# Adaptive modulation in a four-layer diffusion backbone: 32 of 48 weight groups laid out by output column and summed along the row on VectorE, and some weight splits on GpSimd

## The chip, the cores and the metric

The kernel runs on one core of one Trainium2 chip. The metric is the device time of one execution in microseconds (us). The kernel before takes 3222.21 us, the median of three runs (3212.88 to 3223.43).

## What is computed

The reference is one inference step of a backbone of four layers: latent attention (layers 0 and 3), a state-space mixer (layer 1) and gated linear attention (layer 2), on 128 context tokens and 256 latent tokens of width 2048. Around each mixer stands the adaptive modulation, and that is what the change is about:

```
def ada_modulation(cond, w, b):
    m = jax.nn.silu(cond) @ w + b
    shift, scale, gate = jnp.split(m[:, None, :], 3, axis=-1)
    return shift, scale, gate
...
    for l in range(DEPTH):
        shift_p, scale_p, gate_p = ada_modulation(c_ctx[None, :], ada_w[l], ada_b[l])
        shift_s, scale_s, gate_s = ada_modulation(c, ada_w[l], ada_b[l])
        hp = rms_norm(xp, norm_pre[l]) * (1.0 + scale_p) + shift_p
        hs = rms_norm(xs, norm_pre[l]) * (1.0 + scale_s) + shift_s
        ...  (the mixer of the layer: op, os_)
        xp = xp + gate_p * rms_norm(op, norm_post[l])
        xs = xs + gate_s * rms_norm(os_, norm_post[l])
```

`ada_w` is 4 x 2048 x 6144 in float32, 201 MB. Only two condition vectors (c_ctx and c) meet it, so each of its numbers is used twice and then never again. Everything is float32.

## The kernel before, in words

**Dense weights.** Every projection is cut into chunks of four k-tiles (4 x 128 input rows) by 512 columns (384 for q). A chunk is loaded by SyncE into one of four slots of `raw`. ScalarE copies it into `w_hi` in the rounded form fp32r (`split_chunk`, L494), VectorE subtracts to get the rest, `w_lo` (L501), and TensorE runs three matmuls a tile: hi*hi, hi*lo and lo*hi (L347, or L351 for the out jobs and others whose results lie by token). `w_hi` and `w_lo` have two slots each, so ScalarE may fill the slot of chunk n once TensorE is done with chunk n-2. The semaphores are `hi_ready`, `lo_ready` and `chunk_used`. The jobs of layer 0, in order, are q0, ckv0, krope0, gate0, ukv0, out0; of layer 1 u1, gate1, glu1, out1; of layer 2 glr2, qa2, ka2, va2, r0_2, r1_2, qb2, kb2, vb2, r2_2, r3_2, out2; layer 3 repeats layer 0's. Out and gate jobs have 16 chunks.

**Modulation weights.** `ada_w` is 48 groups of 512 columns, each four slices of 1 MB. The slices pass through the same four slots of `raw` as the dense chunks, in an order fixed when the program is built (`ring_order`). SyncE's queue loads strictly in that order, and each load waits until the slot's last user is done (`load_chunk`, L302). There are two ways through:

- Multiplied: 27 groups. TensorE multiplies a slice by the padded conditions (L386, four matmuls of 32 output rows side by side, `pe_ada_part`), ScalarE copies the sums out of bank 4 (`act_ada`), and TensorE turns them so that columns lie on partitions (L401, `pe_ada_turn`). Groups 0 to 15 go at the start and beside q0, the other 11 beside gate1, qa2, ka2, va2, r0_2, vb2 and r2_2 (`ada_after`).
- Summed apart: 21 groups. VectorE multiplies each k-tile by one number per partition and adds to a running sum, once for each condition (L432, `dve_ada_step`: 32 instructions a group), spread over the dense chunks by `summed_apart`. At the end TensorE sums over the partitions and turns, with eight matmuls by a column of ones (L412, `pe_ada_take`). The slot of the last slice is held until then.

VectorE then adds the bias into `mod` (`dve_ada`, L465).

`stream` (L510) gives the order within VectorE and ScalarE for one dense job: for each chunk first the split of the next chunk, then the modulation steps, then what else the stage has (`between`). VectorE and every other engine run strictly in their written order. GpSimd issues DMAs only, and a few memsets.

## Time and profile before

| | |
|---|---|
| median of three runs | 3222.21 us |
| the profiled execution, its own time | 3231.19 us |
| its span (first to last instruction) | 3229.1 us |
| TensorE busy | 3059.2 us, 95% |
| VectorE busy | 1908.1 us, 59% |
| ScalarE busy | 1050.1 us, 33% |
| GpSimd busy | 203.9 us, 6% |
| DMA | 636 MB, mean 197 GB/s |
| TensorE's granted clock, mean | 0.975 of 2.4 GHz |

The span is one execution seen by the hardware profiler, and lies 2.1 us inside that execution's own time. "Busy" for TensorE is a union of overlapping matmuls, and says that work stood there, not that it ran at its peak. VectorE's and ScalarE's instructions hardly overlap, so that their busy time is close to their load; back-to-back instructions start a little earlier than the one before ends. An engine's share is a mean over stages, and the stages differ.

### The profile page before, as it was taken

Reading aid. Unit: us, or ns where it says so; the run is one execution under the profiler, and the core shown is the slowest. Engines: PE = TensorE matmul, PEld = TensorE weight load, DVE = VectorE, ACT = ScalarE, POOL = GpSimd, SP = SyncE. Lnnn points to the kernel's source line nnn. Section 1 sums busy time; section 2 is a strip of 40 time slices with the busy share of each in tenths; the row PEclk is TensorE's granted clock in tenths of the full one; section 3 lists DMA queues with packets and bytes.
Section 4 is the critical chain, followed back from the end, with each engine's and each line's share of the span. In section 5 each row is a group of like instructions: output and inputs, shape, how many; then the busy total and the mean of one; then the engine's idle time right before and its main releaser. Section 6 shows DMA issues by size and latency. Waiting matters only on the chain.

```text
span 3229.1 us, 46744 instructions
## 1 busy us (share of the span) xinstructions
PE 3059.2 (95%) x19631; PEld 2651.0 (82%) x19631; DVE 1908.1 (59%) x2811; ACT 1050.1 (33%) x1409; POOL 203.9 (6%) x321
## 2 busy tenths in 40 slices
PE   5799999999999999889998999999999999999998
PEld 2588889977788989779987877987787999987777
DVE  3499985545767734638775363764475775235443
ACT  1333333233324222232324243324324222323332
POOL 1034340000000210000000000000000000000000
PEclk7899999999999999989999999999999999999999
DMA  9889995411455897866654564555363655431132
GB/s 354 323 309 352 344 334 182 164 49 53 156 183 179 246 257 270 334 244 219 226 183 142 178 220 164 200 205 191 129 226 126 212 196 176 131 95 53 53 131 91
DMA packets 290498, 636.01 MB, mean 197 GB/s; under 512 B 22000, under 2 KB 55424, under 8 KB 281584
## 3 DMA queue, kind: packets, MB, share of 16 engines
q1 hardware_dynamic: 264384, 524.58, 47.4%
q0 software_dynamic: 25904, 108.44, 9.7%
q8 instruction: 154, 2.52, 0.3%
q14 instruction: 56, 0.46, 0.0%
HBM read 561.01 MB, written 71.89 MB: 196 GB/s over the span
## 4 chain that ended last, share of the span: by engine, by line
PE 80%; DMA 7%; DVE 7%; ACT 3%; DVEq 2%; issue 1%; ACTq 1%; POOL 0%; SPq 0%; POOLq 0%
PE bank L347 36%; PE bank L351 21%; DMA raw<-in_ada_w 3%; PE bank L881 3%; PE bank L875 3%; PE bank L386 2%; PE bank L896 2%; DVE w_lo L501 2%; DVE arena L2147 1%; PE bank L922 1%; PE bank L2518 1%; DMA raw<-in_mla_w_in 1%; PE bank L412 1%; DMA raw<-in_s_w_in 1%; PE bank L900 1%
## 5 line engine op out<-in xcount | busy, mean ns | idle before, releaser
L501 DVE TENSOR_TENSOR w_lo<-raw,w_hi 128x2048 fp32r<-128x2048 f32 (+2 forms) x352 | 617.7, 1771 | 697.7 <-ACTq L495 694.2
L494 ACT ACTIVATE w_hi<-raw 128x2048 fp32r<-128x2048 f32 (+2 forms) x352 | 520.4, 1496 | 1246.8 <-PE bank L347 612.7
L347 PE MATMUL bank<-hT_hi,w_hi 128*128 128x384 f32 (+1 forms) x2608 | 898.4, 344 | 22.3 <-ACT scratch L981 7.7
L347 PE MATMUL bank<-hT_lo,w_hi 128*128 128x384 f32 (+1 forms) x2608 | 885.9, 340 | 0.0
L347 PE MATMUL bank<-hT_hi,w_lo 128*128 128x384 f32 (+1 forms) x2608 | 885.8, 340 | 0.0
L347 PEld LDWEIGHTS bank<-hT_hi,w_hi 128*128 128x128 f32 (+1 forms) x2608 | 492.5, 189 | 49.9 <-issue 34.3
L347 PEld LDWEIGHTS bank<-hT_lo,w_hi 128*128 128x128 f32 (+1 forms) x2608 | 492.5, 189 | 1.5 <-issue 0.5
L347 PEld LDWEIGHTS bank<-hT_hi,w_lo 128*128 128x128 f32 (+1 forms) x2608 | 492.2, 189 | 1.4 <-issue 0.6
L351 PE MATMUL bank<-w_hi,hT_hi 128*128 128x512 f32 x1056 | 421.9, 399 | 3.1 <-issue 2.9
L351 PE MATMUL bank<-w_hi,hT_lo 128*128 128x512 f32 x1056 | 418.1, 396 | 0.0
L351 PE MATMUL bank<-w_lo,hT_hi 128*128 128x512 f32 x1056 | 417.9, 396 | 0.0
L566 ACT ACTIVATE arena<-bank 128x512 f32<-128x512 f32 (+6 forms) x285 | 145.4, 530 | 349.6 <-PE bank L386 80.9
L351 PEld LDWEIGHTS bank<-w_hi,hT_hi 128*128 128x128 f32 x1056 | 199.9, 189 | 58.2 <-issue 13.4
L351 PEld LDWEIGHTS bank<-w_hi,hT_lo 128*128 128x128 f32 x1056 | 199.7, 189 | 46.8
L351 PEld LDWEIGHTS bank<-w_lo,hT_hi 128*128 128x128 f32 x1056 | 200.0, 189 | 44.9
L432 DVE SCALAR_TENSOR_TENSOR bank<-raw,silu_pad,bank 128x512 f32<-128x512 f32 x294 | 221.1, 752 | 21.5 <-issue 8.8
L432 DVE SCALAR_TENSOR_TENSOR arena<-raw,silu_pad,arena 128x512 f32<-128x512 f32 x294 | 219.6, 747 | 0.0
L386 PE MATMUL bank<-raw,silu_pad 128*32 128x512 f32 x864 | 122.7, 647 | 34.9 <-DMA raw<-in_ada_w 34.5
L2147 DVE TENSOR_TENSOR arena<-arena 128x896 f32<-128x896 f32 (+1 forms) x128 | 142.4, 1154 | 5.9 <-issue 4.4
L881 PE MATMUL bank<-w_hi,hT_hi 128*128 128x256 f32 x512 | 99.4, 288 | 3.2 <-DVEq L857 1.6
L875 PE MATMUL bank<-hT_hi,w_hi 128*128 128x512 f32 x256 | 86.5, 419 | 8.1 <-DVE hT_hi L1231 4.3
L1241 DVE TENSOR_REDUCE small<-bank 128x1 f32<-128x384 f32 (+1 forms) x96 | 39.1, 463 | 89.2 <-PE bank L900 87.3
(338 smaller groups left out, 2922.1 us busy)
## 6 DMA issues: line engine op xcount, KB each, us to landing
raw<-in_ada_w SPq DMA_DIRECT2D x192, 1024.0 KB, 7.3
raw<-in_mla_w_in SPq DMA_DIRECT2D x64, 768.0 KB, 7.5
raw<-in_gla_w_in SPq DMA_DIRECT2D x48, 1024.0 KB, 7.4
raw<-in_mla_w_in SPq DMA_DIRECT2D x40, 1024.0 KB, 5.3
raw<-in_mla_w_out SPq DMA_DIRECT2D x32, 1024.0 KB, 5.2
raw<-in_s_w_in SPq DMA_DIRECT2D x32, 1024.0 KB, 8.6
s_out_dram<-arena POOLq DMA_DIRECT2D x32, 512.0 KB, 5.8
s_in_dram<-arena POOLq DMA_DIRECT2D x16, 1024.0 KB, 9.6
```

Of the source, the lines that this page charges most:

```text
L347: mm = nc.tensor.matmul(banks[m][0:width, 0:TOK], wp[:, k, at:at + width], hp[:, kt, :], start=(first and n == 0), stop=(last and n == 2))
L351: mm = nc.tensor.matmul(banks[m][:, 0:cols], hp[:, kt, m * P:(m + 1) * P], wp[:, k, 0:cols], start=(first and n == 0), stop=(last and n == 2))
L386: mm = nc.tensor.matmul(banks[4][32 * k:32 * k + 32, :], silu_pad[:, at:at + 32], raw_of("ada", a, s)[:, k, :], start=(s == 0), stop=(s == ...
L432: op = nc.vector.scalar_tensor_tensor(out=raw_of("ada", a, s)[:, c, :] if k == 15 else sums, in0=got, scalar=by, in1=sums, op0=ALU.mult, o ...
L494: nc.scalar.activation(dst, src_, ACT.Copy)
L501: nc.vector.tensor_tensor(dst, src_, pick(w_hi, *part)[0], ALU.subtract)
L566: return nc.scalar.activation(out, in_, ACT.Copy)
L875: mm = nc.tensor.matmul(banks[7][:, 0:KEYS], wp[:, slot, kt, j * 256:j * 256 + P], cp[:, kt, :], start=(kt == 0 and m == 0), stop=(kt == 3 ...
L881: mm = nc.tensor.matmul(banks[7][:, (t % 2) * 256:(t % 2 + 1) * 256], cp[:, kt, t * P:(t + 1) * P], wp[:, slot, kt, :].rearrange("p (h x) ...
L896: nc.tensor.matmul(score_bank(hh, t), qn[:, 2 * pair + hh, at], kT[:, pair % 2, hh, a:b], start=True, stop=False, skip_group_check=True)
L1241: nc.vector.reduce_max(mx[h % 2][:, t:t + 1], score_bank(h, t), AX.X)
L2147: nc.vector.tensor_tensor(to, powers, f, ALU.mult)
```

## The change

Groups 0 to 15 stay as they were, multiplied by TensorE. The other 32, in nine sets of three or four (`summed_sets`), are all treated on VectorE, and in another way:

- The host lays their weights out by output column (`ada_rows`): a partition holds 4 pieces of 512 input rows for one output column and a quarter of the inputs, 8 KB in one stretch. Loading is a plain copy of 1 MB a slice.
- SiLU of the two conditions is written once to DRAM and read back, broadcast over partitions (`pool_silu`), into a place in the arena for each set, or for sets 5 to 7 for one condition into PSUM bank 4.
- VectorE multiplies a piece of 512 by the conditions element by element and sums along the row in the same instruction (`accum_out`), one number per partition: again 32 instructions a group (1024 in all, against 672 L430 and L432 before).
- At the end of a set TensorE adds the four quarters of the inputs, with four matmuls of 32 output rows (`spread`), nine times.
- Five stages (gate0, out0, glu1, out1, out2) have their `w_lo` subtraction on GpSimd for all but the first chunk or two: 15, 15, 14, 15 and 15 chunks, 74 in all (`by_pool`, `pool_splits`).
- ScalarE's last gate copies in layer 0 wait for set 0 to be summed, because the conditions' place lies in the gate's area; GpSimd's `fetch_x` in layer 1 waits for set 3.

```diff
--- before.py
+++ after.py
-ADA_READ = (7, 11, 17, 19, 26, 31, 41, 43, 47)
-ADA_TURNED_APART = (7, 11, 15, 26, 36, 41)
+ADA_TENSOR = 16
+ADA_READ = (7, 11, 15)
...
+    return {("q0", g): ADA_START + g for g in range(ADA_TENSOR - ADA_START)}
+def summed_sets(layers):
+    def chunks(name, first, end):
+        per = chunks_of(name)
+        return [(name, n // per, n % per) for n in range(first, end)]
+    gla = [(f"{name}2", n, s) for name, groups in GLA_ORDER for n in range(groups) for s in range(4)]
+    return [(range(16, 20), chunks("gate0", 0, 16), (13824, 14336, 22144)),
+            (range(20, 23), chunks("out0", 1, 13), (12928, 13632, 13448)),
+            (range(23, 27), chunks("u1", 1, 16) + chunks("gate1", 0, 11), (4608, 5120, 5632)),
+            (range(27, 31), chunks("glu1", 1, 16), (19200, 19712, 20224)),
+            (range(31, 34), chunks("out1", 1, 13), (12928, 13632, 13448)),
+            (range(34, 38), gla[:24], (12928, None, 13448)),
+            (range(38, 41), gla[28:47], (12928, None, 13448)),
+            (range(41, 44), chunks("out2", 1, 13), (12928, None, 13448)),
+            (range(44, 48), chunks("q3", 1, 31), (9216, 9728, 10240))]
...
+    steps, loads, dense = {}, {}, dense_order(layers)
+    for groups, keys, _ in summed_sets(layers):
         for n, a in enumerate(groups):
             for k in range(16):
-                key = keys[(16 * n + k) // pace]
+                key = keys[(16 * n + k) * len(keys) // (16 * len(groups))]
                 steps.setdefault(key, []).append((a, k))
                 if k % 4 == 0:
                     loads.setdefault(dense[dense.index(key) + 1], []).append((a, k // 4))
-            takes[key] = a
...
+            if a >= ADA_TENSOR:
+                load_chunk(sp, "ada", a, s, w["ada_rows"][a // ADA_LAYER, 4 * (a % ADA_LAYER) + s], GC)
+                return
...
-        def pe_ada_take(pe, a):
-            pe.wait_ge(ada_summed, 32 * (SUMMED.index(a) + 1))
-            if a - 1 in ADA_READ:
-                pe.wait_ge(ada_turned, a + ada_reads(a))
-            for c in range(2):
-                for j in range(4):
-                    at = 8 * (a % ADA_LAYER) + 2 * j + c
-                    mm = nc.tensor.matmul(banks[5][:, at:at + 1], raw_of("ada", a, 3)[:, c, j * P:(j + 1) * P], one_col,
-                                          start=True, stop=True)
+        def pe_ada_take(pe, f):
+            groups, _, places = SETS[f]
+            pe.wait_ge(ada_summed, sums_before(groups[-1]) + 33)
+            pe.wait_ge(ada_turned, set_taken(f) - 1)
+            n = 8 * len(groups)
+            for k in range(4):
+                mm = nc.tensor.matmul(banks[5][32 * k:32 * k + 32, 0:n], spread[:, :], sums_of(f)[:, k, 0:n],
+                                      start=True, stop=True, skip_group_check=True)
             mm.then_inc(ada_turned, 1)
+        def sums_of(f):
+            return view(SETS[f][2][2], 4, 32)
+        def silu_of(f, c):
+            at = SETS[f][2][c]
+            return banks[4][:, :] if at is None else view(at, GC)
...
-            n, s, kk = SUMMED.index(a), k // 4, k % 4
-            if kk == 0:
+            s, f = k // 4, SET_OF[a]
+            first = a == SETS[f][0][0]
+            if k % 4 == 0:
                 chunk_landed(nc.vector, "ada", a, s)
-            if k == 0 and a in (16, 44):
-                x_free(nc.vector, a // ADA_LAYER - (a == 16))
-            if k == 0 and a - 1 not in SUMMED:
-                nc.vector.wait_ge(ada_turned, a + ada_reads(a))
-            for c, sums in enumerate((banks[4][:, :], ada_rows(a))):
-                got, by = raw_of("ada", a, s)[:, kk, :], silu_c[:, k, c:c + 1]
-                if n or k:
-                    nc.vector.wait_ge(ada_summed, 32 * n + 2 * k + c - 1)
-                if k == 0:
-                    op = nc.vector.tensor_scalar(sums, got, by, None, ALU.mult)
-                else:
-                    op = nc.vector.scalar_tensor_tensor(out=raw_of("ada", a, s)[:, c, :] if k == 15 else sums, in0=got, scalar=by,
-                                                        in1=sums, op0=ALU.mult, op1=ALU.add)
-                op.then_inc(ada_summed, 1)
+            if k == 0 and first:
+                nc.vector.wait_ge(ada_turned, set_taken(f) - 1)
+                if f in SILU_PLACED:
+                    nc.vector.wait_ge(silu_in, 16 + 64 * (SILU_PLACED[f] + 1))
+            for o in (2 * (k % 4), 2 * (k % 4) + 1):
+                kk, c = ((0, 0), (1, 0), (0, 1), (2, 0), (1, 1), (3, 0), (2, 1), (3, 1))[o]
+                done = sums_before(a) + 8 * s + o
+                if done > (o != 1):
+                    nc.vector.wait_ge(ada_summed, done - (o != 1))
+                got = raw_of("ada", a, s)[:, kk, :]
+                at = 8 * (a - SETS[f][0][0]) + 2 * s + c
+                nc.vector.scalar_tensor_tensor(out=got if c else banks[5][:, :], in0=got, scalar=1.0, in1=silu_of(f, c), op0=ALU.mult,
+                                               op1=ALU.mult, accum_out=sums_of(f)[:, kk, at:at + 1]).then_inc(ada_summed, 1)
+            if k == 15 and a == SETS[f][0][-1]:
+                nc.vector.drain().then_inc(ada_summed, 1)
...
+        def pool_silu(pool, r):
+            c0, c1, _ = SETS[[f for f in SILU_PLACED if SILU_PLACED[f] == r][0]][2]
+            to = view(c0, 2, c1 - c0)[:, :, 0:GC]
+            for q in range(4):
+                nc.gpsimd.dma_start(to[32 * q:32 * q + 32, :, :],
+                                    silu_dram[:, q * GC:(q + 1) * GC].unsqueeze(0).broadcast_to([32, 2, GC])).then_inc(silu_in, 16)
...
+            elif eng == "pool":
+                nc.gpsimd.wait_ge(hi_ready, n + 1)
+                nc.gpsimd.wait_ge(lo_ready, n)
+                for part in parts:
+                    dst, src_ = pick(w_lo, *part)
+                    nc.gpsimd.tensor_tensor(dst, src_, pick(w_hi, *part)[0], ALU.subtract).then_inc(lo_ready, 1)
             else:
                 nc.vector.wait_ge(hi_ready, n + 1)
+                if by_pool(n - 1):
+                    nc.vector.wait_ge(lo_ready, n)
...
+        def by_pool(n):
+            name, g, s = dense[n] if n >= 0 else ("", 0, 0)
+            return 4 * g + s >= {"gate0": 1, "out0": 1, "glu1": 2, "out1": 1, "out2": 1}.get(name, 99)
+        def pool_splits(name, first, end):
+            for n in range(first, end):
+                split_chunk("pool", name, n // 4, n % 4)
...
                     if g == 0:
                         pe_spread_gate(pe, l, s)
+                    if (g, s) == (3, 1) and l != layers[-1]:
+                        pe_ada_take(pe, (1, 4, 7)[l])
...
+                if (l, g) == (0, 3):
+                    act.wait_ge(ada_summed, sums_before(19) + 33)
+                if (l, g) == (3, 0):
+                    act.wait_ge(ada_turned, set_taken(8))
...
+            if l == 2:
+                dve.wait_ge(norm_taken[0], 8 * n + 7)
+                nc.vector.tensor_copy(banks[4][:, :], silu_of(4, 1))
...
             if l != layers[0]:
                 pool.wait_ge(x_added, NT * (parked(l) - 1))
+                if l != 2:
+                    pool_silu(pool, {1: 2, 3: 5}[l])
                 nc.gpsimd.dma_start(x_dram.rearrange("t p d -> p t d"), x).then_inc(x_saved, 16)
                 pool.wait_ge(x_saved, 16 * (parked(l) - 1))
         def fetch_x(pool, l):
             pool.wait_ge(h_lo_ready, h_quarter(f"mix{l}", 3))
+            if l < 2:
+                pool_silu(pool, (1, 4)[l])
+            if l == 1:
+                pool.wait_ge(ada_turned, set_taken(3))
...
+            pool.wait_ge(scanned, 2)
+            pool_silu(pool, 3)
             nc.gpsimd.dma_start(outs[4].rearrange("a b d (g h) n r -> (a b d g) (h n r)", h=2), st_rows)\
                 .then_inc(state_stored, 16)
+            pool_splits(f"glu{l}", 2, 16)
...
+                if l != layers[-1]:
+                    pool_splits(f"out{l}", 1, 2)
                 fetch_x(pool, l)
+                if l != layers[-1]:
+                    pool_splits(f"out{l}", 2, 16)
...
+            if l == 0:
+                x_free(pool, l)
+                pool_silu(pool, 0)
+                pool_splits("gate0", 1, 5)
             pool.wait_ge(kv_normed, nth(l) + 1)
             nc.gpsimd.dma_start(outs[2][0, j], ckv_sb[:, 0, :]).then_inc(stored, 16)
+            if l == 0:
+                pool_splits("gate0", 5, 13)
             pool.wait_ge(kr_taken, nth(l) + 1)
             nc.gpsimd.dma_start(outs[3][0, j], kr_sb[:, 0, 0:ROPE]).then_inc(stored, 16)
+            if l == 0:
+                pool_splits("gate0", 13, 16)
...
+    by_column = arrays["ada_w"].reshape(DEPTH, 4, GC, 48, 4, 32).transpose(0, 3, 1, 5, 4, 2)
+    arrays["ada_rows"] = np.ascontiguousarray(by_column).reshape(DEPTH, 48, P, 4, GC)
```

On TensorE, in gate1 (layer 1), between two dense chunks. L401 and L386 are the turn and the multiplication of a modulation group, L2480 is the state-space mixer's own work, L347 the dense matmuls. Before:

```order
L401 MATMUL bank<-small,arena 128x2 x4
L386 MATMUL bank<-raw,silu_pad 32x512 x4
L2480 MATMUL bank<-arena 64x50 x32
L347 MATMUL bank<-hT_hi,w_hi 128x384
L347 MATMUL bank<-hT_lo,w_hi 128x384
```

And now (L2568 and L357 are the same two lines of code in the changed file):

```order
L2568 MATMUL bank<-arena 64x50 x32
L357 MATMUL bank<-hT_hi,w_hi 128x384
L357 MATMUL bank<-hT_lo,w_hi 128x384
L357 MATMUL bank<-hT_hi,w_lo 128x384
```

The modulation has left the place between the chunks.

On VectorE, in gate0 (layer 0), around one dense chunk late in the stage. L501 is the `w_lo` split, L432 the modulation, L813 to L819 the attention's keys. Before:

```order
L501 TENSOR_TENSOR w_lo<-raw,w_hi 128x2048
L432 SCALAR_TENSOR_TENSOR bank<-raw,silu_pad,bank 128x512
L432 SCALAR_TENSOR_TENSOR arena<-raw,silu_pad,arena 128x512
L432 SCALAR_TENSOR_TENSOR bank<-raw,silu_pad,bank 128x512
L432 SCALAR_TENSOR_TENSOR arena<-raw,silu_pad,arena 128x512
L813 TENSOR_TENSOR arena<-bank,arena 128x256 x2
L816 TENSOR_TENSOR arena<-arena 128x256 x2
L819 TENSOR_TENSOR arena<-arena 128x256 x2
```

And now (L449 is the modulation, L878 to L884 the keys):

```order
L449 SCALAR_TENSOR_TENSOR bank,arena<-raw,arena 128x512 x2
L449 SCALAR_TENSOR_TENSOR raw,arena<-raw,arena 128x512
L449 SCALAR_TENSOR_TENSOR bank,arena<-raw,arena 128x512
L449 SCALAR_TENSOR_TENSOR raw,arena<-raw,arena 128x512
L449 SCALAR_TENSOR_TENSOR bank,arena<-raw,arena 128x512
L449 SCALAR_TENSOR_TENSOR raw,arena<-raw,arena 128x512 x2
L878 TENSOR_TENSOR arena<-bank,arena 128x256 x2
L881 TENSOR_TENSOR arena<-arena 128x256 x2
L884 TENSOR_TENSOR arena<-arena 128x256 x2
```

Eight modulation instructions stand between one chunk's keys and the next, and the split is gone from this engine.

On GpSimd, in layer 0 from the rotary tables on. Before:

```order
L2757 DMA arena<-const_rope_swap 128x128
L2759 DMA out<-arena 128x512
L2761 DMA out<-arena 128x64
L1807 DMA arena<-in_x_prompt 128x2048
L1808 DMA arena<-in_x_sample 128x2x2048
L1800 DMA x_saved_dram<-arena 128x3x2048
```

And now:

```order
L2855 DMA arena<-const_rope_swap 128x128
L470 DMA arena<-silu_dram 32x2x512 x4
L541 ISA
L541 TENSOR_TENSOR w_lo<-raw,w_hi 128x2048 x4
L2861 DMA out<-arena 128x512
L541 TENSOR_TENSOR w_lo<-raw,w_hi 128x2048 x8
L2865 DMA out<-arena 128x64
L541 TENSOR_TENSOR w_lo<-raw,w_hi 128x2048 x4
L470 DMA arena<-silu_dram 32x2x512 x4
L1890 DMA arena<-in_x_prompt 128x2048
L1891 DMA arena<-in_x_sample 128x2x2048
L541 TENSOR_TENSOR w_lo<-raw,w_hi 128x2048 x14
```

The splits of gate0 and out0 stand among the DMA issues, and one of out0's stands ahead of the second group of condition loads.

## Rows read from the trace of the kernel before

**Rows 1.** The page, part 1: busy us, share of the span, instructions.

```profile
PE 3059.2 (95%) x19631; PEld 2651.0 (82%) x19631; DVE 1908.1 (59%) x2811; ACT 1050.1 (33%) x1409; POOL 203.9 (6%) x321
```

**Rows 2.** The page, part 4: the chain of waits, shares by engine.

```profile
PE 80%; DMA 7%; DVE 7%; ACT 3%; DVEq 2%; issue 1%; ACTq 1%; POOL 0%; SPq 0%; POOLq 0%
```

**Rows 3.** Windows (gate0, out0, glu1's stream, out2): length, busy PE, PEld, DVE, ACT, POOL.

```profile
498.10:643.10 145.00, 144.23 (x833) 143.03 (x833) 87.41 (x107) 43.21 (x42) 1.09 (x2) 1.00 0.50 169
815.90:980.40 164.50, 158.09 (x735) 127.98 (x734) 106.64 (x132) 50.14 (x58) 1.27 (x2) 0.98 0.49 173
1446.70:1586.10 139.40, 138.91 (x802) 138.58 (x800) 111.30 (x122) 44.25 (x35) 0.55 (x1) 1.00 0.57 198
2316.00:2467.80 151.80, 147.59 (x689) 121.69 (x688) 99.28 (x114) 45.95 (x46) 0.77 (x1) 0.99 0.51 182
```

**Rows 4.** Timeline of TensorE in gate1: start, length, line, what, count.

```profile
1205.99 0.95 PE L401 MATMUL bank<-small,arena 128*128 128x2 f32 x8
1206.88 1.07 PE L386 MATMUL bank<-raw,silu_pad 128*32 128x512 f32 x8
1207.87 2.07 PE L2480 MATMUL bank<-arena 128*64 128x50 f32 x64
```

**Rows 5.** Timeline of TensorE in out0, between two dense chunks.

```profile
940.61 1.84 PE L412 MATMUL bank<-small,raw 128*128 128x1 f32 x16
942.31 0.48 PE L351 MATMUL bank<-w_hi,hT_hi 128*128 128x512 f32 x1
```

**Rows 6.** Groups by line, VectorE and TensorE: count | busy us, mean ns | idle before.

```profile
L412 PE MATMUL bank<-small,raw 128*128 128x1 f32 x336 | 40.0, 249 | 4.1 <-DVE raw L432 4.1
L501 DVE TENSOR_TENSOR w_lo<-raw,w_hi 128x2048 fp32r<-128x2048 f32 x216 | 495.0, 2292 | 630.0 <-ACTq L495 627.1 <-issue 0.9
L432 DVE SCALAR_TENSOR_TENSOR bank<-raw,silu_pad,bank 128x512 f32<-128x512 f32 x294 | 221.1, 752 | 21.5 <-issue 8.8 <-DMA raw<-in_ada_w 6.4
L432 DVE SCALAR_TENSOR_TENSOR arena<-raw,silu_pad,arena 128x512 f32<-128x512 f32 x294 | 219.6, 747 | 0.0
L2194 DVE SCALAR_TENSOR_TENSOR arena<-arena 128x512 f32<-128x512 f32 x32 | 21.9, 686 | 0.0
```

**Rows 7.** Timeline of VectorE in out0, around one dense chunk.

```profile
918.54 2.29 DVE L501 TENSOR_TENSOR w_lo<-raw,w_hi 128x2048 fp32r<-128x2048 f32 x1 [1.38 <-ACTq L495]
921.02 0.76 DVE L432 SCALAR_TENSOR_TENSOR bank<-raw,silu_pad,bank 128x512 f32<-128x512 f32 x1 [0.19 <-issue]
921.68 0.75 DVE L432 SCALAR_TENSOR_TENSOR arena<-raw,silu_pad,arena 128x512 f32<-128x512 f32 x1
922.35 0.75 DVE L432 SCALAR_TENSOR_TENSOR bank<-raw,silu_pad,bank 128x512 f32<-128x512 f32 x1
```

**Rows 8.** Timelines in out0: two hi splits, and TensorE's first matmul of each chunk.

```profile
916.57 1.92 ACT L494 ACTIVATE w_hi<-raw 128x2048 fp32r<-128x2048 f32 x1 [0.16 <-issue]
924.15 1.92 ACT L494 ACTIVATE w_hi<-raw 128x2048 fp32r<-128x2048 f32 x1 [5.66 <-PE bank L351]
...
923.89 0.39 PE L351 MATMUL bank<-w_hi,hT_hi 128*128 128x512 f32 x1
932.25 0.40 PE L351 MATMUL bank<-w_hi,hT_hi 128*128 128x512 f32 x1
```

**Rows 9.** The lines L1006 and L1814: duration min/median/max ns, first and last start.

```profile
L1006 ACT ACTIVATION_READ_ACCUMULATOR arena<-bank x48: 191/194/195, 873.6 to 3221.5; 128x1 f32 x48
L1814 POOL MEMSET arena<- x1: 1802/1802/1802, 1762.4 to 1762.4; 32x2048 f32 x1
```

**Rows 10.** Timeline of ScalarE at the end of gate0.

```profile
638.87 1.92 ACT L494 ACTIVATE w_hi<-raw 128x2048 fp32r<-128x2048 f32 x1 [6.96 <-PE bank L347]
647.26 0.49 ACT L1056 ACTIVATE arena<-bank 128x384 f32<-128x384 f32 x1 [1.61 <-PE bank L347]
```

**Rows 11.** Timeline of TensorE at the end of glu1.

```profile
1586.28 1.84 PE L412 MATMUL bank<-small,raw 128*128 128x1 f32 x16
1591.03 0.76 PE L351 MATMUL bank<-w_hi,hT_hi 128*128 128x512 f32 x1 [2.91 <-issue]
```

138 lines of the change are left out of this document (76 added, 62 removed).

## The prediction, as it stood before the result

> **What bounds the kernel now.** I read the page's busy shares first: TensorE is busy 95% of the span, VectorE 59%, GpSimd 6% and almost only with DMA issues [rows 1]. Then the chain of waits: 80% of the path that sets the end is TensorE's [rows 2]. Then windows by stage: in gate0, out0, the dense stream of glu1, and out2 TensorE idles 0.8, 6.4, 0.5 and 4.2 us [rows 3]. So every microsecond taken from TensorE in a dense stage counts, as long as nothing else becomes the pacemaker. Who is next can be read from the same windows: VectorE, with 87 of 145, 107 of 165, 111 of 139 and 99 of 152 us [rows 3].
>
> **What leaves TensorE.** Eleven groups are no longer multiplied there. In gate1 the multiplication of one slice holds TensorE from 1206.88 to 1207.87, 1.0 us, and the turn of a group from 1205.99 to 1206.88, 0.9 us [rows 4]: 11 x (4 x 1.0 + 0.9) = 54 us. The 21 takes (336 records, 16 each [rows 6]) go too: the dense matmul behind one starts 1.70 us after it [rows 5], and two of them also waited for VectorE, 4.1 us in all: 21 x 1.7 + 4 = 40 us. Nine new takes of four matmuls come in, nearest to the turn: 9 x 0.9 = 8 us. Net 54 + 40 - 8 = 86 us, all on the path. ScalarE's eleven copies go as well, off the path.
>
> **What the new VectorE instruction costs.** Before, the instructions of L432 start 0.66 us apart (921.02, 921.68, 922.35 [rows 7]) and last 752 ns, pointer scalar included; one without such a scalar lasts 686 ns [rows 6], which makes 0.60 apart. The sum has to be read out in addition, and no row of VectorE shows that. From below it costs nothing; from above I take ScalarE's readout, 194 ns [rows 9], on top of the slower form: 0.60 to 0.86 us. I take 0.75. The new chain also waits once in eight for the instruction just ahead, 0.2 us as behind a split [rows 7]. A slice is thus 8 x 0.75 + 0.2 = 6.2 us, and gate0, out0, out1 and out2 have one a chunk, glu1 slightly more.
>
> **What the split costs on GpSimd.** It is 2292 ns on VectorE [rows 6]; there are 74 that move. GpSimd has no such instruction in the trace. Its memset of 2048 numbers takes 1802 ns [rows 9], so one stream of that length costs it 1.8 us; a subtraction has two coming in and one going out. Ends: 1.8 us (all three side by side) and 5.4 us (one after another). I take 4.5, nearer the upper end, as two inputs surely share something. The time there is for it: in out0 the hi split that starts at 916.57 ends at 918.49 and TensorE takes up that chunk at 923.89, 5.4 us later, and the next has 926.07 to 932.25, 6.2 us [rows 8]. The first is the case in which ScalarE was held by its squares. So 4.5 us fits beside TensorE with 0.8 us over, and the upper end just fits too. Without this cover every microsecond over some 5.5 to 6.2 would cost one for each of the 74 chunks.
>
> The Trainium skill (GPSIMD Engine Reference, 3.1 Elementwise) has this subtraction's like, two inputs of 2048 float32, at 4497 ns. No row here shows it. By that page the sum would be what it is.
>
> **VectorE's pace where it is tightest.** In out0 a chunk takes TensorE 8.36 us (923.89 to 932.25 [rows 8]). VectorE's own work there is 106.6 - 16 x 2.29 - 64 x 0.66 = 28 us, 1.7 a chunk [rows 3]; 6.2 + 1.7 = 7.9 us, just under. In gate0: 87.4 - 16 x 2.29 - 52 x 0.66 = 16 us, 1.0 a chunk; 7.2 us under 8.9 (145 us less two takes, by 16). In the other sets a chunk has 4.3 to 5.3 modulation instructions and keeps its split, about what it had. Unevenness within the out stages should still cost something: 0.86 us apart instead of 0.75 is 0.9 us a chunk, 0.4 over. I charge 5 us.
>
> **New waits.** (a) End of gate0: the hi split of the next job ends at 640.79 [rows 10], VectorE's split of it then ends near 643.1 and the last slice near 649.4; only then may ScalarE make its four last gate copies (2 us, so 651.4, against 647.75 before [rows 10]). Behind them in ScalarE's queue is the split of the latents that TensorE waits for: 3.7 us. (b) End of glu1: VectorE has eight or nine instructions of 0.75 behind its last split where it had six of 0.66, 2.3 us more, and behind them stands the gating that out1's first chunk needs; TensorE already waited there until 1591.03 [rows 11]: 2 us. (c) At the start of the out jobs GpSimd splits a chunk, then issues up to six DMAs at 0.6 us, then splits the next: 2 us in out0, less elsewhere. (d) The loads of SiLU lie ahead of x's in GpSimd's queue, and VectorE waits for them before its first step of a set; a slice waits in its slot, so I allow 2 us. SyncE gains a little: the slot of a group's last slice comes free with VectorE and no longer with TensorE. Sum of costs: 5 + 4 + 2 + 2 + 2 = 15 us.
>
> **The sum.** 3231.2 (the profiled execution's own time; its span is 2.1 less) - 86 + 15 = 3160 us. That execution stood 9 us above the median of 3222.2, so in the median's terms 3151.
>
> **The rivals.**
>
> 1. *VectorE and GpSimd get in each other's way; slower than before.* Each new modulation instruction reads two inputs from SBUF, and so does each split that moves. If the two engines reach SBUF through something they share, and an instruction holds it from start to end, the times add. Then a chunk costs VectorE 6.2 + 4.5 = 10.7 us. Out0 and out1: eight chunks at 8.36 and four at about 10.2, 2.3 x 8 + 0.5 x 4 = 20 each. Gate0: 10.7 + 1.0 - 8.9 = 2.8, by 15: 42. Glu1: 11.1 - 8.4 = 2.7 by 14, and the gating (three of 1.75): 42. Out2, with one condition's numbers in PSUM, may hide one instruction a chunk: 13. Together 137 us: 3151 + 137 = 3288. It decides from the point where 6.2 plus what is taken away exceeds a chunk, 2.2 us of the 4.5. For it: a two-input instruction needs twice the reading, and VectorE is loaded in just these five stages. Against: nothing in the trace; GpSimd's DMA issues show no stretch, but they do not read tiles. This is the largest risk.
>
> The Trainium skill (SBUF — State Buffer, "SBUF: two separate sides") states just this: whichever of a VectorE instruction with two SBUF inputs and a GpSimd instruction that reads SBUF starts first has the pair of ports to itself until it ends. By that rule the case above holds in full. No run here has yet shown it.
>
> 2. *The readout makes the new instruction much dearer*, about 1.2 us: twice 512 elements' time, (0.60 + 0.53). Then 9.8 us a slice; by the same chunks, out0, out1 and out2 some 20 each, gate0 31, glu1 31, and q3, where 128 such instructions stand beside 32 splits in 233 us, 19: 141 us and 3292. For it: there is no row. Against: two SBUF inputs alone do not do it (L432 takes 747 ns with both in SBUF, 752 with one in PSUM [rows 6]).
>
> The Trainium skill (Vector Engine (DVE) Microarchitecture Reference, 7. Points that are easy to get wrong) says that this form with two sources that are not bf16 in SBUF halves the throughput, since nothing is left to read the accumulator back. No row here has an accumulating instruction on VectorE, so this rival rests on it.
>
> 3. *GpSimd is slower than I take*, 6.5 to 7 us a split: 74 x 0.5 to 1.2 = 37 to 90 us given back, 3190 to 3240, around no change. For it: the interleaving with six DMA issues and fp32r output. Against: one stream costs 1.8 us.
>
> **How the numbers follow.** Forecast 0.48; rival 1 0.34; rival 2 0.05; rival 3 0.09; some other small net effect 0.04. The range of the forecast alone is 3135 to 3185, from 0.60 and 0.86 us for the instruction and none or twice the waits. For 8 in 10 the range has to reach rivals 1 and 3: 3138 to 3305; rival 1's own width (0.60 to 0.86 us, 3.6 to 5.4 us) is 3240 to 3350, so that its upper part is left out. A measurement of this kernel tells 0.3%, 10 us, from no change. Faster by more: 0.48 + 0.02 + 0.02 = 0.52. Slower by more: 0.34 + 0.05 + 0.03 = 0.42. The same: 0.06. I set the time at 3155, 4 us above the sum, for waits I have not found.
>
> **What the profile after would show.** TensorE: no L386 behind q0, nine takes of about 0.9 us, chunks of out0 8.36 us apart where no take stands. VectorE: the new instruction with its readout, 0.75 us from pair to pair. GpSimd: splits of 4.5 us that do not change when VectorE is busy, and VectorE's instructions the same in gate1 (no split on GpSimd) as in gate0. If instead the modulation instructions in the five stages show single ones of several microseconds, or GpSimd's splits stretch when VectorE runs, rival 1 holds; if all of them last 1.2 us, in q3 too, rival 2. If SyncE's loads in out0 wait for VectorE and ScalarE's hi splits wait for a DMA, VectorE has become the pacemaker there, and the forecast is wrong.

## The result, and the profile after

The changed kernel takes 3259.83 us (median of four runs, 3255.62 to 3261.70) against 3217.55 us for the kernel before beside it: ratio 1.0133, 95% interval 1.0107 to 1.0159. The forecast was 3155 us: 2% faster was foretold, and the kernel is 1.3% slower. The time lies inside the range (3138 to 3305), on the side of rival 1.

The page after, part 1 (answers to [rows 1]):

```profile
PE 2958.5 (91%) x18927; PEld 2594.9 (80%) x18927; DVE 2190.0 (67%) x4117; ACT 1043.5 (32%) x1399; POOL 570.3 (18%) x420
```

TensorE is busy for 101 us less. The span grew by 29 us all the same (3258.5 against 3229.1; by the medians it is 42, the profiled execution of the kernel before being 14 us above its median), so TensorE's idle time grew by 130. The chain of waits, which was 80% TensorE's [rows 2], shows who took over:

```profile
PE 58%; DVE 24%; DMA 8%; ACT 4%; issue 2%; DVEq 2%; ACTq 1%; POOL 1%; SPq 0%; POOLq 0%
```

Windows after of gate0, out0, glu1 (whole) and out2, columns as in [rows 3]:

```profile
488.20:648.70 160.50, 147.42 (x821) 144.24 (x820) 155.62 (x276) 42.65 (x40) 71.69 (x17) 0.97 0.57 203
824.90:1010.60 185.70, 155.75 (x711) 126.71 (x711) 129.37 (x246) 50.14 (x58) 75.61 (x21) 0.93 0.50 178
1320.60:1594.80 274.20, 234.99 (x3111) 218.48 (x3109) 206.69 (x510) 85.65 (x108) 72.19 (x21) 0.95 0.68 256
2361.60:2513.70 152.10, 143.83 (x673) 119.80 (x672) 116.69 (x226) 45.92 (x47) 70.77 (x16) 0.97 0.58 209
```

The columns are: the window and its length, busy time of PE, PEld, DVE, ACT and POOL, the granted clock, the DMA share and GB/s. Length minus TensorE's busy time is its idle time: 13 us in gate0 (0.8 before), 30 in out0 (6.4), 39 in glu1 (22.7, also for the whole stage), 8 in out2 (4.2). VectorE is busy 97% of gate0. Now one chunk of out0: VectorE, then GpSimd in the same microseconds (answers to [rows 7]).

```profile
900.77 0.70 DVE L449 SCALAR_TENSOR_TENSOR bank<-raw,arena 128x512 f32<-128x512 f32 x1
901.39 0.14 DVE L449 DVE_READ_ACCUMULATOR bank<-raw,arena 128x1 f32 x1
901.39 0.69 DVE L449 SCALAR_TENSOR_TENSOR raw<-raw,arena 128x512 f32<-128x512 f32 x1
902.00 5.10 DVE L449 SCALAR_TENSOR_TENSOR bank<-raw,arena 128x512 f32<-128x512 f32 x1
907.02 0.13 DVE L449 DVE_READ_ACCUMULATOR bank<-raw,arena 128x1 f32 x1
907.02 0.68 DVE L449 SCALAR_TENSOR_TENSOR raw<-raw,arena 128x512 f32<-128x512 f32 x1
...
911.45 4.92 DVE L449 SCALAR_TENSOR_TENSOR bank<-raw,arena 128x512 f32<-128x512 f32 x1
```

```profile
901.50 5.04 POOL L541 TENSOR_TENSOR w_lo<-raw,w_hi 128x2048 fp32r<-128x2048 f32 x1 [6.15 <-ACTq L534]
910.70 5.11 POOL L541 TENSOR_TENSOR w_lo<-raw,w_hi 128x2048 fp32r<-128x2048 f32 x1 [4.16 <-ACTq L534]
```

The same instruction takes 0.69 us alone and 5.10 us when it starts while a split runs: it ends about 0.6 us after the split does, its own time. It goes the other way too. The split at 901.50 started while VectorE's instruction of 901.39 was still running (to 902.08), and ended 4.46 us after it. Of the 74 splits 54 started during a modulation instruction with both inputs in SBUF, and from the end of that one to the end of the split it is 4.46 us in the median. So whichever starts second waits for the first. But such an instruction lasts 0.7 us and a split 4.6, so VectorE pays nearly all of it. That is rival 1 in one picture. By groups (count | busy us, mean ns):

```profile
L449 DVE SCALAR_TENSOR_TENSOR bank<-raw,arena 128x512 f32<-128x512 f32 x512 | 505.3, 987 | 59.3 <-DMA arena<-silu_dram 23.0 <-DMA raw<-in_ada_rows 19.9 <-issue 11.4
L449 DVE SCALAR_TENSOR_TENSOR raw<-raw,arena 128x512 f32<-128x512 f32 x352 | 305.0, 884 | 4.1 <-issue 0.4
L449 DVE SCALAR_TENSOR_TENSOR raw<-raw,bank 128x512 f32<-128x512 f32 x160 | 106.2, 682 | 3.6 <-issue 0.5
L541 POOL TENSOR_TENSOR w_lo<-raw,w_hi 128x2048 fp32r<-128x2048 f32 x74 | 354.0, 4784 | 649.9 <-ACTq L534 649.9
```

The two forms with both inputs in SBUF have means of 987 and 884 ns; the one whose second input is in PSUM stays at 682. Of the 864 of the two forms 53 last over 2 us, at most one for each of the 74 splits: 12 in gate0, 8 in out0, 13 in glu1, 11 in out1 and 9 in out2. Against the medians VectorE spends 219 us more on them. The split costs 4.78 us on the average, its waits included; 4.5 was assumed.

There is a second loss, which no rival named. TensorE's waits in layer 2, 1879 to 2092 and 2233 to 2362 us (us, times, longest), where the kernel before had none and GpSimd splits nothing:

```profile
PE bank L1514 <- DVEq L1766: 18.1, 2, 9.2
PE bank L361 <- DVEq L550: 11.7, 6, 3.6
...
PE bank L1514 <- DVEq L1766: 19.2, 2, 9.7
```

L1766 is the linear attention's decayed keys. They stand behind a chunk's modulation steps on VectorE. L550 is the end of a `w_lo` split on VectorE, in va2.

### The profile page after: what moved, and what is told of

Same layout as the page of the kernel before. It is cut to its first block, busy times and chain, and to the rows that moved or that the text cites. A ratio compares the mean times of both kernels' runs of the same rounds, so it can differ in the third digit from the quotient of the medians.

```text
span 3258.5 us, 46791 instructions
## 1 busy us (share of the span) xinstructions
PE 2958.5 (91%) x18927; PEld 2594.9 (80%) x18927; DVE 2190.0 (67%) x4117; ACT 1043.5 (32%) x1399; POOL 570.3 (18%) x420
## 4 chain that ended last, share of the span: by engine, by line
PE 58%; DVE 24%; DMA 8%; ACT 4%; issue 2%; DVEq 2%; ACTq 1%; POOL 1%; SPq 0%; POOLq 0%
PE bank L357 28%; PE bank L361 12%; DVE bank L449 10%; DVE raw L449 5%; DMA raw<-in_ada_w 3%; PE bank L946 3%; PE bank L940 3%; DVE w_lo L549 2%; PE bank L961 2%; PE bank L987 1%; DMA raw<-in_ada_rows 1%; PE bank L2606 1%; ACT w_hi L533 1%; PE bank L965 1%; DVE arena L2230 1%
## 5 line engine op out<-in xcount | busy, mean ns | idle before, releaser
L357 PE MATMUL bank<-hT_hi,w_hi 128*128 128x384 f32 (+1 forms) x2608 | 889.2, 341 | 33.8 <-POOL w_lo L541 11.2
L357 PE MATMUL bank<-hT_hi,w_lo 128*128 128x384 f32 (+1 forms) x2608 | 878.4, 337 | 0.0
L357 PE MATMUL bank<-hT_lo,w_hi 128*128 128x384 f32 (+1 forms) x2608 | 878.1, 337 | 0.0
L549 DVE TENSOR_TENSOR w_lo<-raw,w_hi 128x2048 fp32r<-128x2048 f32 (+3 forms) x278 | 448.1, 1632 | 444.7 <-ACTq L534 441.0
L449 DVE SCALAR_TENSOR_TENSOR bank<-raw,arena 128x512 f32<-128x512 f32 x512 | 505.3, 987 | 59.3 <-DMA arena<-silu_dram 23.0
L357 PEld LDWEIGHTS bank<-hT_hi,w_hi 128*128 128x128 f32 (+1 forms) x2608 | 493.7, 189 | 53.9 <-issue 23.3
L357 PEld LDWEIGHTS bank<-hT_lo,w_hi 128*128 128x128 f32 (+1 forms) x2608 | 493.5, 189 | 1.2
L357 PEld LDWEIGHTS bank<-hT_hi,w_lo 128*128 128x128 f32 (+1 forms) x2608 | 493.0, 189 | 1.1
L541 POOL TENSOR_TENSOR w_lo<-raw,w_hi 128x2048 fp32r<-128x2048 f32 x74 | 354.0, 4784 | 649.9 <-ACTq L534 649.9
L449 DVE SCALAR_TENSOR_TENSOR raw<-raw,arena 128x512 f32<-128x512 f32 x352 | 305.0, 884 | 4.1 <-issue 0.4
L624 ACT ACTIVATE arena<-bank 128x512 f32<-128x512 f32 (+5 forms) x274 | 138.9, 527 | 363.8 <-PE bank L394 63.4
L449 DVE SCALAR_TENSOR_TENSOR raw<-raw,bank 128x512 f32<-128x512 f32 x160 | 106.2, 682 | 3.6 <-issue 0.5
L394 PE MATMUL bank<-raw,silu_pad 128*32 128x512 f32 x512 | 75.0, 670 | 33.3 <-DMA raw<-in_ada_w 32.6
```

The costliest lines, as they stand in the source:

```text
L357: mm = nc.tensor.matmul(banks[m][0:width, 0:TOK], wp[:, k, at:at + width], hp[:, kt, :], start=(first and n == 0), stop=(last and n == 2))
L394: mm = nc.tensor.matmul(banks[4][32 * k:32 * k + 32, :], silu_pad[:, at:at + 32], raw_of("ada", a, s)[:, k, :], start=(s == 0), stop=(s == ...
L449: nc.vector.scalar_tensor_tensor(out=got if c else banks[5][:, :], in0=got, scalar=1.0, in1=silu_of(f, c), op0=ALU.mult, op1=ALU.mult, acc ...
L541: nc.gpsimd.tensor_tensor(dst, src_, pick(w_hi, *part)[0], ALU.subtract).then_inc(lo_ready, 1)
L549: nc.vector.tensor_tensor(dst, src_, pick(w_hi, *part)[0], ALU.subtract)
L624: return nc.scalar.activation(out, in_, ACT.Copy)
```

## Experiments

| kernel | median us | ratio to before, 95% interval |
|---|---|---|
| changed kernel | 3259.8 | 1.0133, 1.0107 to 1.0159 |
| no_pool | 3188.6 | 0.9934, 0.9916 to 0.9953 |
| gla_late | 3227.3 | 1.0058, 1.0038 to 1.0079 |
| both | 3162.9 | 0.9858, 0.9834 to 0.9882 |
| psum_both | 3200.0 | 0.9952, 0.9932 to 0.9971 |
| before_pool | 3188.2 | 0.9939, 0.9919 to 0.9958 |
| before_pad | 3179.1 | 0.9908, 0.9887 to 0.9929 |
| pad_first | 3200.4 | 0.9969, 0.9957 to 0.9980 |
| pad_64 | 3200.4 | 0.9965, 0.9950 to 0.9979 |
| both_thin | 3109.4 | 0.9685, 0.9655 to 0.9715 |
| psum_late | 3145.6 | 0.9801, 0.9783 to 0.9819 |
| paced | 3143.6 | 0.9791, 0.9768 to 0.9815 |

The kernel before took 3209.6 to 3211.7 us beside them.

**no_pool: the splits back on VectorE.**

```diff
-            return 4 * g + s >= {"gate0": 1, "out0": 1, "glu1": 2, "out1": 1, "out2": 1}.get(name, 99)
+            return False
...
-                split_chunk("pool", name, n // 4, n % 4)
+                if by_pool(chunk(name, n // 4, n % 4)):
+                    split_chunk("pool", name, n // 4, n % 4)
```

> All 74 w_lo subtractions go back from GpSimd to VectorE; the modulation stays as changed. Theory (VectorE and GpSimd hold a shared way to SBUF in turn): the splits take 2.29 us again instead of 4.7, no modulation instruction lasts over 0.8 us (75 of them lasted 4 to 5.1 us before), and TensorE's idle time in gate0, out0, glu1, out1 and out2 falls from 114 us to about 50; near 3200 us, 60 below the changed kernel's 3260. Rival (VectorE is simply overloaded in those stages by eight modulation instructions a chunk, and GpSimd was a relief): 74 x 2.29 = 170 us more work on VectorE, a chunk then costs it 8 x 0.61 + 2.29 + 1 to 1.7 = 8.2 to 8.9 us against TensorE's 8.2, and the time is the changed kernel's or up to 30 us more, 3260 to 3290.

Measured 3188.6, 71 us less. All 864 instructions with two SBUF inputs (min/median/max ns):

```profile
L449 DVE SCALAR_TENSOR_TENSOR bank<-raw,arena x512: 690/697/703, 496.6 to 2657.4; 128x512 f32<-128x512 f32 x171
L449 DVE SCALAR_TENSOR_TENSOR raw<-raw,arena x352: 678/685/694, 498.0 to 2660.9; 128x512 f32<-128x512 f32 x176
```

Not one is held. VectorE was given 74 splits more and was less busy (2116.7 us against 2190.0). TensorE's idle time in the five stages fell from 114 to 52 us; 50 was expected. The rival, plain overload, falls. (The expectation's count of 75 long instructions is wrong: 53 modulation instructions last over 2 us, 48 of them over 4.)

**gla_late: in layer 2's jobs the modulation behind the mixer's work.**

```diff
-                    for a, k in steps[early:]:
+                    late = name[-1] == "2" and name[:3] != "out"
+                    for a, k in steps[early:] if not late else []:
                         dve_ada_step(a, k)
                     if between:
                         between(g, s)
+                    for a, k in steps[early:] if late else []:
+                        dve_ada_step(a, k)
```

> In the jobs of layer 2 other than out2 VectorE does the modulation steps of a chunk behind the mixer's own work of that chunk (decayed and the like) instead of ahead of it; GpSimd's splits stay. Theory (there the order on VectorE makes TensorE wait, a second cause beside the sharing): TensorE's waits for L1766 (37 us) and in va2 for L550 (12 us) go to under 10 us together; 35 us less than the changed kernel, near 3225. Rival (all of the loss is the sharing in the five stages; the waits in layer 2 would only move to the next instruction, since VectorE has the same amount to do): within 10 us of the changed kernel, 3250 to 3270.

Measured 3227.3, 33 us less. The waits for the decayed keys went from 37 to 10 us (L1769 here, two rows of waits of 1830 to 2110 and one of 2214 to 2327 us); those of va2 stayed, 11 against 12 us, so that half of the theory was wrong. In va2 it is the amount, not the order: when `paced` (below) takes steps out of va2, these waits fall to 5 us.

```profile
PE bank L361 <- DVEq L550: 11.0, 6, 2.4
PE bank L1517 <- DVEq L1769: 6.2, 2, 3.9
...
PE bank L1517 <- DVEq L1769: 3.9, 2, 2.0
```

**both: the two edits together.**

> Both edits at once. If the two causes are apart, the savings add: 60 + 35 = 95 us less than the changed kernel, near 3165 and some 50 us under the kernel before; TensorE's idle time outside of the waits that the kernel before had is then near 40 us. Rival (one pacemaker behind both, VectorE's total work): the savings don't add and the time is within 15 us of the better one of the two alone, near 3200.

Measured 3162.9: 97 us less, against 71 + 33 = 104 of the two alone. The savings add to within 7 us, so there are two causes.

**psum_both: GpSimd keeps its splits, the conditions move to PSUM.** For sets 0, 1, 3 and 7:

```diff
+            if f in IN_PSUM:
+                return banks[5 - c][:, :]
...
+                if f in IN_PSUM:
+                    for c_ in range(2):
+                        if SETS[f][2][c_] is not None:
+                            nc.vector.tensor_copy(banks[5 - c_][:, :], view(SETS[f][2][c_], GC))
+                    nc.vector.drain()
...
-                nc.vector.scalar_tensor_tensor(out=got if c else banks[5][:, :], in0=got, ...
+                nc.vector.scalar_tensor_tensor(out=got if c else dump_of(f), in0=got, ...
```

> The changed kernel with its splits on GpSimd, but in gate0, out0, glu1 and out2 the two conditions' SiLU lie in PSUM (banks 4 and 5), so that no modulation instruction there has two inputs in SBUF; what each throws away goes to SBUF. out1 stays as it was, as the control. Theory (what is held is a VectorE instruction with two SBUF inputs beside a GpSimd split): modulation instructions over 2 us vanish in the four stages and stay in out1 (27 to 30 of them); TensorE's idle time falls in gate0 from 13 to 1 to 3, out0 from 30 to about 9, glu1 from 39 to about 20, out2 from 8 to about 5 us and stays at 24 in out1; near 3205 us against 3260. Rival (GpSimd holds up every VectorE instruction that touches SBUF, wherever the second input lies, or VectorE is just full): within 15 us of 3260, instructions of 4 to 5 us in all five stages.

The first two lines are in `silu_of`. What the instruction throws away goes to SBUF instead of bank 5 (`dump_of`).

Measured 3200.0, 60 us less. The modulation by form:

```profile
L460 DVE SCALAR_TENSOR_TENSOR raw<-raw,bank x336: 661/682/690, 497.1 to 2427.8; 128x512 f32<-128x512 f32 x168
L460 DVE SCALAR_TENSOR_TENSOR bank<-raw,arena x288: 682/696/5100, 1009.6 to 2665.6; 128x512 f32<-128x512 f32 x144
L460 DVE SCALAR_TENSOR_TENSOR arena<-raw,bank x224: 674/684/690, 495.8 to 2426.6; 128x512 f32<-128x512 f32 x112
L460 DVE SCALAR_TENSOR_TENSOR raw<-raw,arena x176: 677/686/5135, 1011.0 to 2669.1; 128x512 f32<-128x512 f32 x176
```

With one input in PSUM the longest of 560 lasts 690 ns, though 158 of them ran from start to end inside a split. Here is one split in out0 and VectorE at its start; five such instructions follow one another 0.61 us apart while it runs, and the split keeps its 4.6 us:

```profile
881.38 4.62 POOL L552 TENSOR_TENSOR w_lo<-raw,w_hi 128x2048 fp32r<-128x2048 f32 x1 [6.15 <-ACTq L545]
```

```profile
881.21 0.68 DVE L460 SCALAR_TENSOR_TENSOR raw<-raw,bank 128x512 f32<-128x512 f32 x1
881.82 0.68 DVE L460 SCALAR_TENSOR_TENSOR arena<-raw,bank 128x512 f32<-128x512 f32 x1
882.43 0.68 DVE L460 SCALAR_TENSOR_TENSOR raw<-raw,bank 128x512 f32<-128x512 f32 x1
```

The stages' lengths in us:

| stage | before | changed | no_pool | psum_both |
|---|---|---|---|---|
| gate0 | 145.0 | 160.5 | 142.3 | 139.4 |
| out0 | 164.5 | 185.7 | 164.7 | 169.3 |
| glu1, whole | 260.4 | 274.2 | 250.5 | 249.1 |
| out1, the control | 147.8 | 161.6 | 152.0 | 168.0 |
| out2 | 151.8 | 152.1 | 155.7 | 145.9 |

The four stages with the conditions in PSUM lose 69 us together; out1 does not fall (it is 6 us longer, which is not explained) and keeps its 25 us of idle time and all 9 modulation instructions over 2 us that are left (27 to 30 were expected there; the changed kernel itself has 11). This is the strongest of the runs on the cause: the engines and the sums stayed as they were, only the place of one input and of the thrown-away output changed. The output is not the cause: the form that writes `raw` in SBUF is held with two SBUF inputs (5135 ns) and not with one (690).

**before_pool: the splits on GpSimd, with the old modulation.**

It also has before_pad's 128 unused bytes, so that before_pad, below, is what it is compared with.

> The kernel before, padded by 128 bytes as in before_pad (3179 us), with the five stages' splits on GpSimd and its own modulation kept: of its two multiply-adds a k-tile one has its running sum in PSUM, the other in SBUF. Theory of sharing: of L432's two forms only arena<-raw,silu_pad,arena is ever held (over 2 us), bank<-raw,silu_pad,bank stays at 0.75 us; a chunk of out0 costs VectorE 4 to 5 x 0.66 + 1.7 + 4.4 = 9 us against TensorE's 8.2, so the kernel is 5 to 40 us slower than before_pad, 3185 to 3220. Rival (GpSimd only relieves VectorE, which has time to spare here): 3170 to 3180, no instruction over 1 us.

Measured 3188.2, 9 us over before_pad, at the edge of what these runs can tell (the two intervals overlap). VectorE in out0, beside a split that GpSimd runs from 829.52 to 834.07:

```profile
829.59 0.75 DVE L433 SCALAR_TENSOR_TENSOR bank<-raw,silu_pad,bank 128x512 f32<-128x512 f32 x1
830.24 4.38 DVE L433 SCALAR_TENSOR_TENSOR arena<-raw,silu_pad,arena 128x512 f32<-128x512 f32 x1
834.54 0.74 DVE L433 SCALAR_TENSOR_TENSOR bank<-raw,silu_pad,bank 128x512 f32<-128x512 f32 x1
```

The sum in PSUM passes a running split, the sum in SBUF waits for it. So moving these splits does not pay with the old modulation either.

**before_pad, pad_first, pad_64: why every dense matmul became quicker.** Each adds one unused tensor to the kernel before: `sb("spread", [P, 32])` after `small`, `sb("pad", [P, 32])` ahead of `raw`, `sb("spread", [P, 16])` after `small`.

> The kernel before with one more tensor of 128 bytes a partition, which nothing uses, at the place where the changed kernel has its spread matrix; every later tensor moves by 128 bytes. Question: why dense matmuls start 227 ns apart in the changed kernel against 232 before, in stages that the change does not touch too. Theory (the place of the operands in SBUF): 227 ns (173.5 instead of 175.9 for 384 columns) and 30 to 40 us less than the kernel before, near 3180. Rival (less is written and read beside them, or the two profiled executions differ): 232 ns and within 5 us of the kernel before.

> The kernel before with the 128 unused bytes ahead of all tensors instead of between the weights' buffers and the activations: everything moves by 128 bytes, so the distance from w_hi and w_lo to hT_hi and hT_lo is that of the kernel before. Theory A (what counts for the matmuls' pace is how the two operands lie to each other): 232 ns a matmul of 512 columns as before, 3210 us. Theory B (what counts is where the activations lie by themselves): 227 ns and 3179 us, as in before_pad. Theory C (where the weights lie also matters): something else than either.

> The kernel before with 64 unused bytes ahead of the activations instead of 128. The distance from the weights' buffers to hT is then 64 more than a multiple of 128 bytes (0 before, and with 128 bytes of padding a multiple of 256). Theory 1 (only a distance that is an odd multiple of 128 bytes is bad): 227 ns a matmul of 512 columns and near 3180 us. Theory 2 (only a multiple of 256 bytes is good): 232 ns or slower, 3200 to 3215 us.

Two successive chunks of out3, 36 matmuls of 512 columns each, of before_pad, pad_first and pad_64:

```profile
3136.23 0.39 PE L352 MATMUL bank<-w_hi,hT_hi 128*128 128x512 f32 x1
3144.39 0.39 PE L352 MATMUL bank<-w_hi,hT_hi 128*128 128x512 f32 x1
```

```profile
3153.77 0.39 PE L352 MATMUL bank<-w_hi,hT_hi 128*128 128x512 f32 x1
3162.14 0.39 PE L352 MATMUL bank<-w_hi,hT_hi 128*128 128x512 f32 x1
```

```profile
3151.22 0.39 PE L352 MATMUL bank<-w_hi,hT_hi 128*128 128x512 f32 x1
3159.46 0.39 PE L352 MATMUL bank<-w_hi,hT_hi 128*128 128x512 f32 x1
```

A chunk takes 8.16 us (227 ns a matmul), 8.37 (232, as before [rows 8]) and 8.24 (229). Moving everything by 128 bytes leaves the pace as it was; moving the activations and not the weights changes it. That fits theory A, by which it counts how the two operands lie to each other. The time is less clear: theory A forecast 3210 us for pad_first, which has the old pace and is still 11 us faster than before. In the traces its half-clock total (the stretches in which the granted clock is 0.5, added up) is 120 us against 165; why is open. With 64 bytes the pace lies between, and both theories of that run fail as stated.

**both_thin: the change with VectorE's part nearly free.** The modulation works on `[:, 0:8]` of each operand; the instructions last 158 to 174 ns. It leaves out 504 of every 512 products, so its sums are not the modulation; the loads, waits and takes stay. The splits are on VectorE and the late order holds, as in `both`.

> The version with all splits on VectorE and the late steps in layer 2 (both, 3163 us), with each of the 1024 modulation instructions over 8 of its 512 elements: the sums are left out, the loads, waits and takes stay. It asks what the change was worth had VectorE's part been nearly free. Theory (the TensorE step of the forecast was right, 86 us, and what ate it is VectorE's time): the kernel before at the same placing (3179) less 86 is 3093; allowing 10 us for the takes' and loads' own waits, 3090 to 3105. Rival (TensorE's part was worth less than 86, because the sums are replaced by waits for loads and by the takes): 3120 to 3160.

Measured 3109.4: 70 us less than the kernel before at the same placing, not the 74 to 89 expected, and well under the rival. By the traces TensorE's busy time fell by 88 us (3016.2 in before_pad, 2928.4 here), and its idle time rose by 15 (161.0 and 176.1).

**psum_late and paced.** The first joins psum_both and gla_late and takes `"out1": 1` out of `by_pool`; the second deals group 34 to 37's steps by weight: `[k for k in gla[:24] for _ in range({"qa": 3, "ka": 2, "va": 1}.get(k[0][:2], 3))]`.

> The same, with out1's splits back on VectorE and the modulation steps of layer 2's jobs behind the mixer's own work: all causes found so far taken away, while 59 splits stay on GpSimd. Theory: the savings add, 3260 - 55 - 35 - 12 = 3158 us, level with or a few us under the version without any split on GpSimd (3163). Rival (VectorE's other instructions with two SBUF inputs, the keys, the gatings and the splits of hT, are held too and cost as much as GpSimd relieves): 3175 to 3190.

> The best version so far (psum_late, 3146 us) with the steps of groups 34 to 37 dealt out by the time a chunk has: qa 3, ka 2, va 1, r0_ and r1_ 3 shares instead of one each. Theory (in va2, VectorE 88% busy, TensorE waits 10 us because too many steps stand in chunks of 9 us): TensorE's idle time in ka2 and va2 falls from 13.5 to under 4 us, that in r0_ and r1_ stays under 6; 3135 to 3140. Rival (the wait moves with the steps into the r jobs, whose VectorE work has waits of its own): 3143 to 3150.

psum_late measured 3145.6, 12 us better than expected: 2% under the kernel before, with 59 splits on GpSimd. No modulation instruction is held (longest 702 ns), and now the splits do pay: 17 us less than `both`, which has them on VectorE. Against no_pool, whose five stages hardly differ from those of `both`, 10 us of it are in out2 (145.7) and 3 in gate0 (139.4), while out0 is 2 us longer (166.8). The PSUM places alone, with the splits on VectorE, were not run.

paced measured 3143.6, which cannot be told from psum_late. Its windows of ka2, va2, r0_ and r1_ (length, busy, clock):

```profile
1766.40:1812.50 46.10, 42.66 (x216) 36.85 (x215) 36.83 (x65) 19.36 (x12) 0.00 (x0) 1.00 0.43 158
1812.50:1885.90 73.40, 70.08 (x329) 56.92 (x330) 61.56 (x92) 29.14 (x26) 1.44 (x2) 0.98 0.45 170
1885.90:1946.40 60.50, 56.64 (x306) 46.57 (x306) 40.38 (x88) 23.14 (x36) 2.86 (x4) 0.92 0.41 152
1946.40:2006.70 60.30, 57.65 (x303) 47.34 (x301) 39.51 (x90) 17.84 (x27) 2.88 (x4) 0.92 0.45 165
```

The idle time did fall (3.3 us in va2, against 10.0), though ka2 and va2 together keep 6.8 and not under 4. The two stages took 14 us less (119.5 against 133.8). But r0_ and r1_ ran at a granted clock of 0.92 where psum_late has 0.97, and took 6.5 us longer at hardly more idle time (6.5 against 6.1 us); neither theory had that, and why the clock was lower is open. The rest of the gain was lost ahead of ka2, which starts 8 us later than in psum_late.

## Why the prediction was wrong, point by point

**The step that failed** is the overlap of VectorE and GpSimd in "VectorE's pace where it is tightest". The forecast set a chunk of out0 at 6.2 + 1.7 = 7.9 us of VectorE, "just under" TensorE's 8.36, with the 4.5 us split beside it, and charged VectorE nothing for that split. The runs show that a modulation instruction which starts during a split waits for that split's end: 53 of them lasted over 2 us, and VectorE's instructions took 219 us longer in all. Having the splits on GpSimd costs 71 us (no_pool). Rival 1's mechanism was named, priced and had its rule of the chip beside it, and was given 0.34 against 0.48. "Against: nothing in the trace" was the true state of the evidence, yet it was read as a reason for the forecast. The trace before could not decide, because GpSimd read no tile in it, and then the one written rule that speaks to the case should have carried the forecast. The Trainium skill (SBUF — State Buffer, "SBUF: two separate sides") has it in full; runs here agree: 5.10 us beside a split, 0.69 alone, 0.68 with an input in PSUM.

**Rival 1's price** was 137 us over the forecast. What it costs is 71 us by no_pool, and 60 for four of the five stages by psum_both. By stage length against no_pool, out0 was right (20 forecast, 21 measured); gate0 and glu1 were priced at 42 each and lost 18 and 24, out1 10 instead of 20, and out2, priced at 13, is 4 us shorter. That the measured 3260 lies only 28 us from rival 1's 3288 is partly luck: the price was nearly twice what was measured, and costs outside of it (33 us for the order in layer 2, 31 more than charged for VectorE's time), less the placing, filled most of the gap. What was mis-sized is the slice: 8 x 0.61 us and no wait for the accumulator, 4.9 us, not 6.2; with 4.4 us held and 1.0 of its own a chunk of gate0 comes to 10.3 where 11.7 was reckoned (VectorE's busy time there is 155.6 / 16 = 9.7). And not every split holds a step: 53 of 74. (The split's slack in out0 was also misadded, 5.40 less 4.5 being 0.9 and not 0.8 us; nothing hangs on it.)

**TensorE's 86 us** was right: its busy time falls by 88 in both_thin. That both_thin as a whole gained 70 us, where the sum says 86 - 15 = 71, is luck. Of the 15 us of waits 5, 4 and 2 were to come from VectorE's time and 2 from GpSimd's splits, and both_thin has hardly any of the first and none of the last, yet TensorE idles 15 us more.

**"Just under" a chunk** was not free. psum_late has the splits on GpSimd, nothing held in the modulation and the late order, so it is the case that the forecast had in mind, and it lies 36 us above both_thin. Five were charged. In the traces (41 us apart) 29 of it is idle time of TensorE, 205 against 176 us, and 12 is more busy time. The half clock goes with the idle time: the stretches at 0.5 add up to 183 us in psum_late, 152 in both_thin, 281 in the changed kernel and 165 before, whose idle times are 205, 176, 300 and 170. One of them: in out0 of psum_late TensorE waits 6.8 us for VectorE, until 851.87, and the granted clock is 0.5 from 848.6 to 855.5. At 0.5 matmuls of 512 columns start 427 ns apart, at 1.0 227 (both in psum_late). So idle time of TensorE can cost more than its own length.

**"In the other sets a chunk keeps its split, about what it had"** failed in layer 2, in amount and in order. In qa2, ka2 and va2 VectorE had no modulation at all before (no L432 between 1769 and 1858 us), and in va2 its load now makes TensorE wait 12 us for the splits (L550). And the order was not reckoned: in the kernel before, the groups of qa2, ka2, va2, r0_2, vb2 and r2_2 were on TensorE, and VectorE had nothing ahead of the decayed keys there. The order cost 33 us (gla_late).

**What it lacked: the placing**, 31 us to the good (before_pad), by a tensor of 128 bytes. If the changed kernel owes it as much, it would have been 73 to 81 us slower than the kernel before without it; that kernel was not run. How much of the 31 is the matmuls' pace is not settled either, since pad_first gained 11 us at the old pace.

From the kernel before, all in us: -31 placing, -70 TensorE's work less the small waits, +36 VectorE's time for the sums, +33 order in layer 2, +71 to 82 for holding (no_pool; psum_late to the changed kernel, less the order): 39 to 50 in all, and 50 were measured against the 3210 beside the experiments (42 in the first comparison). With the upper value the terms are steps from one run to the next, so that they add up to 50 of themselves; the independent one, no_pool's 71, leaves 11 us open.

**Rivals 2 and 3** are refuted: the accumulating instruction starts every 0.61 us with its readout beside the next, so that the halved throughput on which rival 2 rested is not borne out here, and the split takes 4.5 to 5.1 us.

## What to carry to other kernels

Before work moves to GpSimd, list what VectorE runs beside it with two inputs in SBUF, and put one of the two in PSUM: in four stages that won back 60 us, and with out1's splits back on VectorE a move that had lost 71 us won 17. When work moves onto an engine, look at what then stands behind it in that engine's order, not only at the sum of its load. And when a change adds a small tensor, time the kernel before with the same tensor unused, or its placing will be taken for the change's doing.
